# Differential attention on one core: the score pieces of the two maps issued strictly in turn

## The chip, the cores and the metric

The kernel runs on one core of a Trainium2 chip. The metric is the device time of one execution in microseconds (us). The core has a matrix engine (TensorE, in the profile PE for its matmuls and PEld for the loading of its stationary operand), a vector engine (VectorE, DVE), a scalar engine (ScalarE, ACT), GpSimd (POOL), and SyncE (SP), which issues the DMAs. They run side by side and wait for one another by semaphores. SBUF holds operands, PSUM receives what TensorE computes; it has eight banks of 512 float32 values on each of 128 partitions.

## What is computed

One layer of a hybrid network on 128 context tokens and 1024 latent tokens, d_model 1024, all in float32: a SwiGLU feed-forward half step, then differential attention (4 heads, two maps of 64 dimensions each) beside an RG-LRU group, an output projection, and a second feed-forward half step. The attention is this part of the reference:

```python
def block(qi):
    s = jnp.einsum('bqhmd,bkhmd->bhmqk', qi, k, preferred_element_type=jnp.float32) * scale
    p = jax.nn.softmax(s, axis=-1)
    pd = p[:, :, 0] - lam * p[:, :, 1]
    return jnp.einsum('bhqk,bkhv->bqhv', pd.astype(v.dtype), v)
```

A block of 128 queries of one head has two maps of scores, m = 0 and m = 1, each with its own 64 dimensions of the query and the key. Context queries see the 128 context keys; latent queries see 1024 latent keys and 128 keys of a cache.

## The kernel before

All engines run programs written out by hand; the order of the work on each engine is the order of the text, and semaphores tie them together. The feed-forward halves, the projections and the attention follow one another. The attention is the stretch from 1273 to 1508 us of the profile.

It goes over 36 units, u = 0 to 35: for each of four heads one unit of context queries (128 keys) and eight units of latent queries (1152 keys, `UNIT`). For a latent unit `scores(u)` issues six matmuls, which are those of `PIECES`: tuples of map, first key and last key. I call them A1, A2 (map 0, 512 keys each), A3 (map 0, the 128 keys of the cache), and B1, B2, B3 for map 1. In the kernel before their order is A1, A2, B1, A3, B2, B3. In the profile each of these matmuls is two pairs of a weight load and a matmul, so a latent unit has 12 of each; the cache's pieces read `sb_kc`, the others only `sb_x`.

Map 0's operands lie on partitions 0 to 63 and its matmuls are placed at rows 0 to 63 of the array (`tile_position=(m * DH, 0)`), map 1's at rows 64 to 127. Map 0 writes PSUM banks 0 to 2, map 1 banks 3 to 5. There is one set of these banks for all units: ahead of A1 the kernel waits until the exponentials of map 0 of the unit before have been read out of them, ahead of B1 for those of map 1 (`e_done`). After A3 and after B3 `s_ready` is raised.

One pass of the loop on TensorE is: `scores(u)`; then for unit u-2 three transposes of its probabilities, `group(u-2, 0)` (L694); for unit u-3 five blocks of `values` (L708, twice as many records); three more transposes, four more blocks of values, and the last three transposes. The transposes share PSUM bank 6, so each group waits for ScalarE's copy of the one before (`t_done`). ScalarE's pass is: copy of the first transposes of u-2 (L1029), the exponentials of map 0 of unit u (L1036, with the reading of its accumulator as an instruction of its own), second copy, the exponentials of map 1 of unit u, third copy, and the squares of an output (L1044). VectorE's pass is: the maximum over the scores of map 0, that of map 1 (both L1393), the weighted difference of the probabilities of unit u-1 (L1399, L1400, L1402), and the output of u-3 (L1408).

Of the kernel before, what the change touches and what calls it, by code (L numbers as in the profile page):

```python
# [43 lines left out]
GROUP0 = [0] + [1 + 3 * t for t in range(9)]  # L44
GROUPS = GROUP0[9]
UNIT = LAT + 128
PIECES = ((0, 0, 512), (0, 512, 1024), (1, 0, 512), (0, 1024, UNIT), (1, 512, 1024), (1, 1024, UNIT))
MIX_ORDER = (4, 5, 6, 7, 0, 1, 2, 3)
LAM_INIT = 0.8 - 0.6 * math.exp(0.0)
KEYS = T + 128  # L50
# [22 lines left out]
def build(nc, a, out):  # L73
    ctx = ExitStack()
    with ctx:
# [349 lines left out]
        def _(pe):  # L425
# [244 lines left out]
            def scores(u):  # L670

                hd, q = u // QT, u % QT
                for m, b, e in ((0, 0, P), (1, 0, P)) if q == 0 else PIECES:
                    if b == 0 and 2 * u + m > 1:
# [885 lines left out]
```

## Time and profile before

| | |
|---|---|
| runs | 2498.46, 2496.99, 2494.31 us; median 2496.99 |
| the profiled execution | 2498.43 us, of which the span from the first to the last instruction is 2496.6 us |
| attention, 1273 to 1508 us | some 235 us, 36 units |
| PE busy over the span | 2396.6 us (96%) |
| DVE, ACT, POOL busy | 1128.3, 668.6, 29.7 us |
| mean granted TensorE clock | 0.978 |

The profile is one execution. Matmuls are pipelined: a record lasts longer than the distance from one matmul to the next, and a busy PE isn't a PE at its peak. Where the timeline merges records of a kind, "x7" is their number, and the time is that in which at least one of them ran. The bracket at the end of a row tells how long the engine was idle before it, and who released it. The chain of waits follows the end back from what released what.

### The profile page before, as it was taken

Reading aid. Unit: us, or ns where it says so; the run is one execution under the profiler, and the core shown is the slowest. Engines: PE = TensorE matmul, PEld = TensorE weight load, DVE = VectorE, ACT = ScalarE, POOL = GpSimd, SP = SyncE. Lnnn points to the kernel's source line nnn. Section 1 sums busy time; section 2 is a strip of 40 time slices with the busy share of each in tenths; the row PEclk is TensorE's granted clock in tenths of the full one; section 3 lists DMA queues with packets and bytes.
Section 4 is the critical chain, followed back from the end, with each engine's and each line's share of the span. In section 5 each row is a group of like instructions: output and inputs, shape, how many; then the busy total and the mean of one; then the engine's idle time right before and its main releaser. Section 6 shows DMA issues by size and latency. Waiting matters only on the chain.

```text
span 2496.6 us, 35528 instructions
## 1 busy us (share of the span) xinstructions
PE 2396.6 (96%) x14392; PEld 2236.1 (90%) x14392; DVE 1128.3 (45%) x1845; ACT 668.6 (27%) x1174; POOL 29.7 (1%) x36
## 2 busy tenths in 40 slices
PE   5999999999999998999989988999999999999997
PEld 3799999999999987777977768979999999999996
DVE  3544333443334436465557773364443344443335
ACT  3411111111111124465236663251111111111112
POOL 0000000000000000000010030000000000000000
PEclk8999999999999999999989999999999999999998
DMA  9222022210222103111100010111101110101102
GB/s 372 85 75 77 18 83 84 77 74 20 81 84 82 44 1 119 34 34 41 43 21 20 29 46 18 59 52 34 50 22 46 50 50 34 49 22 46 50 9 77
DMA packets 45817, 144.52 MB, mean 58 GB/s; under 512 B 5808, under 2 KB 13360, under 8 KB 45744
## 3 DMA queue, kind: packets, MB, share of 16 engines
q1 hardware_dynamic: 45744, 143.49, 16.7%
q8 instruction: 53, 0.87, 0.1%
q14 instruction: 20, 0.16, 0.0%
HBM read 133.50 MB, written 9.97 MB: 57 GB/s over the span
## 4 chain that ended last, share of the span: by engine, by line
PE 90%; DVE 4%; ACT 3%; DMA 1%; issue 1%; SPq 0%; ACTq 0%; DVEq 0%
PE ps L433 27%; PE ps L435 26%; PE ps L434 26%; PE ps L679 4%; PE ps L708 2%; PE ps L632 2%; DVE sb_tmp L1191 1%; PE ps L694 1%; DVE sb_hL L1183 1%; PE ps L460 1%; DMA sb_stage<-in_w_mod 1%; ACT sb_pr L1036 1%; PE ps L445 1%; PE ps L453 0%; PE ps L470 0%
## 5 line engine op out<-in xcount | busy, mean ns | idle before, releaser
L433 PE MATMUL ps<-sb_hH,sb_guH 128*128 128x384 f32 x2112 | 716.2, 339 | 9.8 <-DVE sb_hL L1183 6.3
L435 PE MATMUL ps<-sb_hH,sb_guL 128*128 128x384 f32 x2112 | 708.0, 335 | 0.0
L434 PE MATMUL ps<-sb_hL,sb_guH 128*128 128x384 f32 x2112 | 708.0, 335 | 0.0
L433 PEld LDWEIGHTS ps<-sb_hH,sb_guH 128*128 128x128 f32 x2112 | 398.0, 188 | 33.7 <-issue 17.4
L1255 DVE SCALAR_TENSOR_TENSOR sb_x<-ps,sb_mod,sb_x 128x128 f32<-128x128 f32 (+1 forms) x704 | 345.9, 515 | 180.9 <-PE ps L435 178.7
L434 PEld LDWEIGHTS ps<-sb_hL,sb_guH 128*128 128x128 f32 x2112 | 398.4, 189 | 0.7 <-issue 0.3
L435 PEld LDWEIGHTS ps<-sb_hH,sb_guL 128*128 128x128 f32 x2112 | 398.3, 189 | 0.0
L1242 DVE TENSOR_TENSOR sb_tmp<-ps,sb_tmp 128x384 f32<-128x384 f32 x132 | 73.5, 557 | 670.6 <-PE ps L435 669.3
L433 PE MATMUL ps<-sb_hidH,sb_dnH 128*128 128x384 f32 x1056 | 356.4, 338 | 0.5 <-DVE sb_x L1255 0.4
L435 PE MATMUL ps<-sb_hidH,sb_dnL 128*128 128x384 f32 x1056 | 353.2, 334 | 0.0
L434 PE MATMUL ps<-sb_hidL,sb_dnH 128*128 128x384 f32 x1056 | 353.1, 334 | 0.0
L895 ACT ACTIVATE sb_hidH<-sb_tmp 128x384 fp32r<-128x384 f32 x132 | 69.3, 525 | 542.4 <-DVE sb_tmp L1242 542.4
L433 PE MATMUL ps<-sb_hH,sb_wiH 128*128 128x384 f32 x576 | 201.6, 350 | 8.3 <-DVE sb_wiL L1104 5.9
L433 PEld LDWEIGHTS ps<-sb_hidH,sb_dnH 128*128 128x128 f32 x1056 | 198.2, 188 | 4.9 <-DVE sb_x L1255 1.0
L892 ACT ACTIVATE sb_tmp<-ps 128x384 f32<-128x384 f32 x132 | 64.4, 488 | 507.0 <-PE ps L435 507.0
L434 PEld LDWEIGHTS ps<-sb_hidL,sb_dnH 128*128 128x128 f32 x1056 | 198.3, 188 | 0.3
L435 PEld LDWEIGHTS ps<-sb_hidH,sb_dnL 128*128 128x128 f32 x1056 | 198.3, 188 | 0.0
L434 PE MATMUL ps<-sb_hL,sb_wiH 128*128 128x384 f32 x576 | 195.9, 340 | 0.0
L435 PE MATMUL ps<-sb_hH,sb_wiL 128*128 128x384 f32 x576 | 195.8, 340 | 0.0
L1104 DVE TENSOR_TENSOR sb_guL<-sb_raw,sb_guH 128x1024 fp32r<-128x1024 f32 x88 | 104.8, 1222 | 66.9 <-ACT sb_guH L795 66.9
L433 PEld LDWEIGHTS ps<-sb_hH,sb_wiH 128*128 128x128 f32 x576 | 110.5, 192 | 16.6 <-issue 5.8
L1393 DVE TENSOR_REDUCE sb_nmx<-ps 128x1 f32<-128x1152 f32 (+1 forms) x72 | 86.3, 1234 | 59.5 <-PE ps L679 58.5
(152 smaller groups left out, 2228.0 us busy)
## 6 DMA issues: line engine op xcount, KB each, us to landing
sb_raw<-in_w_gate SPq DMA_DIRECT2D x44, 512.0 KB, 4.5
sb_raw<-in_w_up SPq DMA_DIRECT2D x44, 512.0 KB, 3.7
sb_raw<-in_w_mod SPq DMA_DIRECT2D x44, 512.0 KB, 4.1
sb_raw<-in_w_down SPq DMA_DIRECT2D x44, 512.0 KB, 4.4
sb_stage<-in_w_mod SPq DMA_DIRECT2D x7, 2048.0 KB, 18.6
sb_raw<-in_w_in SPq DMA_DIRECT2D x16, 512.0 KB, 4.0
sb_x<-in_x SPq DMA_DIRECT2D x3, 1536.0 KB, 10.5
x_spilled<-sb_x SPq DMA_DIRECT2D x8, 576.0 KB, 5.5
```

Of the source, the lines that this page charges most:

```text
L433: pe.matmul(o, wH, xH, start=begin, stop=False)
L434: pe.matmul(o, wH, xL, start=False, stop=False)
L435: return pe.matmul(o, wL, xH, start=False, stop=end)
L632: m = pe.matmul(ps[r, 6 + n % 2, 0:CH], gw[r, w], x[r, XC[j % 2], chunk(c)], start=True, stop=True, tile_position=(r.start, r.start))
L679: mm = pe.matmul(unit(u, m)[:, b:e], x[r, hd, q * P:(q + 1) * P], keys, start=True, stop=True, tile_position=(m * DH, 0))
L708: m = pe.matmul(ps[:, 7, 0:P], pT[:, u % 2, k], vk, start=k == 0, stop=k == nk - 1)
L892: act.activation(tmp[:, b], ps[:, gate_bank(f, c, first)[0], 0:CH], ACT.Silu).then_inc(s["silu"], 1)
L895: act.activation(hidH[:, f, chunk(c)], tmp[:, 2 + b], ACT.Copy).then_inc(s["hidhi"], 1)
L1104: dve.tensor_tensor(dst, raw[:, slot], hi.bitcast(F32), ALU.subtract).then_inc(raw_used[slot], 1)
L1242: dve.tensor_tensor(tmp[:, 2 + b], ps[:, gate_bank(f, c, first)[1], 0:CH], tmp[:, b], ALU.mult).then_inc(s["prod"], 1)
L1255: m = dve.scalar_tensor_tensor(x[:, t, b:e], ps[:, 4 + (c * KT + t) % 3, b - c * CH:e - c * CH], mod[:, gate + t, cond:cond + 1], x[:, t, ...
L1393: dve.tensor_reduce(nmx[:, u % 2, m:m + 1], unit(u, m), AX.X, ALU.max, negate=True).then_inc(mx_ready, 1)
```

## The change

One tuple of constants is reordered. The matmuls, their operands, the PSUM banks and the semaphores are the same; the wait ahead of B1, which stays tied to B1, now stands ahead of A2 as well.

```diff
-PIECES = ((0, 0, 512), (0, 512, 1024), (1, 0, 512), (0, 1024, UNIT), (1, 512, 1024), (1, 1024, UNIT))
+PIECES = ((0, 0, 512), (1, 0, 512), (0, 512, 1024), (1, 512, 1024), (0, 1024, UNIT), (1, 1024, UNIT))
```

In the letters above: A1, A2, B1, A3, B2, B3 becomes A1, B1, A2, B2, A3, B3. The four context units, with one piece for each map, are untouched.

## Rows read from the trace of the kernel before

**Rows 1.** The page: busy time by engine, and the chain's shares by line.
```profile
PE 2396.6 (96%) x14392; PEld 2236.1 (90%) x14392; DVE 1128.3 (45%) x1845; ACT 668.6 (27%) x1174; POOL 29.7 (1%) x36
PE ps L433 27%; PE ps L435 26%; PE ps L434 26%; PE ps L679 4%; PE ps L708 2%; PE ps L632 2%; DVE sb_tmp L1191 1%; PE ps L694 1%; DVE sb_hL L1183 1%; PE ps L460 1%; DMA sb_stage<-in_w_mod 1%; ACT sb_pr L1036 1%; PE ps L445 1%; PE ps L453 0%; PE ps L470 0%
```

**Rows 2.** The chain in the attention, in order of time: start us, us, what.
```profile
1305.95 2.86 PE ps L679 x11
...
1365.63 2.86 PE ps L679 x11
...
1371.68 2.86 PE ps L679 x11
...
1477.01 2.86 PE ps L679 x11
```

**Rows 3.** Timeline of one latent unit: start us, us, engine, line, instruction, count [idle before].
```profile
1366.02 0.22 ACT L1036 ACTIVATION_READ_ACCUMULATOR sb_pr<-ps,sb_nmx 128x1 f32 x1
...
1367.38 0.38 PE L679 MATMUL ps<-sb_kc,sb_x 64*128 64x128 f32 x2
...
1367.80 2.62 DVE L1393 TENSOR_REDUCE sb_nmx<-ps 128x1 f32<-128x1152 f32 x2 [1.38 <-PE ps L679]
1368.11 0.38 PE L679 MATMUL ps<-sb_kc,sb_x 64*128 64x128 f32 x2
...
1368.42 0.31 PEld L694 LDWEIGHTS ps<-sb_ident,sb_pr 128*128 128x128 f32 x3
...
1369.00 0.49 ACT L1029 ACTIVATE sb_pT<-ps 128x384 f32<-128x384 f32 x1 [2.10 <-PE ps L694]
1369.39 1.21 ACT L1036 ACTIVATE sb_pr<-ps,sb_nmx 128x1152 f32<-128x1152 f32 x1
...
1370.95 1.23 ACT L1036 ACTIVATE sb_pr<-ps,sb_nmx 128x1152 f32<-128x1152 f32 x1
```

**Rows 4.** Weight loads of that unit, from short stretches of the timeline.
```profile
1365.56 0.29 PEld L679 LDWEIGHTS ps<-sb_x 64*128 64x128 f32 x2 [0.17 <-issue]
...
1366.29 0.18 PEld L679 LDWEIGHTS ps<-sb_x 64*128 64x128 f32 x1
...
1366.39 0.32 PEld L679 LDWEIGHTS ps<-sb_x 64*128 64x128 f32 x2
...
1366.96 0.19 PEld L679 LDWEIGHTS ps<-sb_kc,sb_x 64*128 64x128 f32 x1
1367.25 0.19 PEld L679 LDWEIGHTS ps<-sb_x 64*128 64x128 f32 x1
...
1368.11 0.19 PEld L679 LDWEIGHTS ps<-sb_kc,sb_x 64*128 64x128 f32 x1 [0.24 <-issue]
```

**Rows 5.** Timeline of the scores of the first latent unit of a head.
```profile
1334.35 2.09 PE L679 MATMUL ps<-sb_x 64*128 64x512 f32 x8
1336.17 0.49 PE L679 MATMUL ps<-sb_kc,sb_x 64*128 64x128 f32 x4
...
1336.59 0.31 PEld L694 LDWEIGHTS ps<-sb_ident,sb_pr 128*128 128x128 f32 x3
```

**Rows 6.** Timeline of the second and third latent units of that head.
```profile
1342.44 2.62 DVE L1393 TENSOR_REDUCE sb_nmx<-ps 128x1 f32<-128x1152 f32 x2 [2.26 <-PE ps L679]
...
1343.84 1.22 ACT L1036 ACTIVATE sb_pr<-ps,sb_nmx 128x1152 f32<-128x1152 f32 x1
...
1345.33 2.26 PE L679 MATMUL ps<-sb_x 64*128 64x512 f32 x6
...
1346.46 0.18 PEld L679 LDWEIGHTS ps<-sb_x 64*128 64x128 f32 x1
```

**Rows 7.** Line 679 from 1358 us on: durations in ns, shortest, median and longest.
```profile
L679 PE MATMUL ps<-sb_x x164: 272/589/693, 1359.5 to 1483.9; 64*128 64x512 f32 x156, 64*128 64x128 f32 x8
```

**Rows 8.** Busy time by stretch: PE, PEld, DVE, ACT, POOL, then granted clock, DMA share, GB/s.
```profile
1277.66:1301.60 23.94, 19.43 (x53) 11.85 (x51) 12.29 (x16) 8.91 (x16) 3.69 (x2) 0.57 0.01 2
1352.80:1356.20 3.40, 3.40 (x11) 2.11 (x8) 1.13 (x1) 0.33 (x3) 0.00 (x0) 0.50 0.00 0
```

## Prediction

> **What bounds the kernel now.** I read the page first. TensorE is busy 96% of the span and carries nearly all of the chain; the scores of the attention (L679) are 4% of it [rows 1]. The change touches these alone, so the question lies in the attention. The chain there shows a pass of 6.05 us for a latent unit (1371.68 less 1365.63; 6.04 by the finer records): 2.86 us of scores and the rest transposes and values, all put down to PE [rows 2]. Read alone, this says that a shorter block of scores shortens the pass one for one. The timeline and the loads say something else, and the prediction rests on the difference.
>
> First, how long do the scores need? The pieces of the two maps sit in different rows of the array. In the first latent unit of a head all eight halves of 512 columns ran within 2.09 us, the four cache halves began 1.82 us after the start, and the next transposes came 2.24 us after it [rows 5]. The halves of one map follow each other by 0.43 us: the second half of A2 is loaded at 1366.53 (1366.39 + 0.32 less a load of 0.18), the first half of A3 at 1366.96 [rows 4]. Eight of them one after another would take 8 x 0.43 = 3.4 us. So in this unit the two maps already run side by side throughout, in the old order, with both 512-column pieces of map 0 ahead of B1 in the text.
>
> Second, why is the usual block 2.86 us and not 2.24? In the unit at 1365.56 the two loads of A1 fall within 0.29 us; a single load starts at 1366.29, 0.73 us after A1, and two more within the 0.32 us from 1366.39 [rows 4]. The load at 1366.29 is that of B1: ScalarE's reading of the accumulator, which ends the exponentials of map 1 of the unit before and frees B1's banks, ended at 1366.02 + 0.22 = 1366.24 [rows 3], 0.05 us ahead. It isn't held by A2, whose second half is loaded later. The kinds of the loads confirm that one map passes the other: a cache load (A3) at 1366.96, then one of 512 columns (of map 1) at 1367.25, and the last cache load (B3) at 1368.11 [rows 4]. B1 is late by a wait on ScalarE, and the profile shows no idle time for it because A1 keeps PE busy.
>
> Third, what closes the pass. From B1 at 1366.29 the stream of map 1 runs to the transposes at 1368.42; then come the first copy on ScalarE at 1369.00, the exponentials of map 0 at 1369.39, a second copy, and the exponentials of map 1 from 1370.95 [rows 3]. Their accumulator read ends one pass after the last one, 1366.24 + 6.04 = 1372.28, and 0.05 us later the next B1 can start: 1372.33, just 6.04 us after 1366.29. ScalarE closes the loop, and B1's start is its other end.
>
> **The change part by part.** It removes and adds no instruction, no transfer and no wait, and no queue but TensorE's has anything moved. Three things move.
>
> B1 is issued ahead of A2. It can't start earlier: in the usual unit it starts 0.05 us after the event it waits for, and that event hangs on ScalarE's chain, which the change doesn't shorten. In the unit at 1334.35, where nothing holds it, both maps end together already. Gain 0.
>
> B2 is issued ahead of A3; B3 stays last. In the free unit the four cache halves take 0.49 us [rows 5] where the two of one map take 0.38 [rows 3], so map 1 ends 0.11 us behind map 0. If that is B2 standing too far back, 0.11 us of TensorE goes away; but what ends late in this unit is ScalarE's work on map 0. Gain 0 to 0.11 us in each of three such units, 0.3 in all; I take 0.
>
> A2 now stands behind B1's wait. Queued with it are B2, A3, B3 and the transposes; who waits for A2 and A3 is VectorE's maximum of map 0, and then the exponentials of map 0. Today A2's second half is loaded at 1366.53, one step of 0.43 after its first half, which is thus loaded at 1366.10 and runs from 1366.53. After the change its load comes behind the two of B1, which are 0.10 apart (1366.29, 1366.39): at 1366.50 at the best. It is in time but not hidden: a first matmul, whose load is uncovered, lasts 693 ns and the others 589 [rows 7], 0.10 us for the load. So A2 is late by 1366.50 + 0.10 - 1366.53, some 0.1 us. Lower bound 0 (it starts when it did); upper bound 0.3 us, if A2 gets in only with B1's second half, 0.43 + 0.10 us after B1, at 1366.82. What covers it: the two maxima run from 1367.80 for 2.62 us, the first to some 1369.15, and the exponentials that need it start at 1369.39, held by the first copy [rows 3]. Less a hand-over of 0.04 the cover is 0.20 us. A delay of 0.1 costs nothing here. At 0.3 it costs 0.10 us in each unit of this pattern, which is the chain's block of 2.86 us, seen from 1305.95 to 1477.01 [rows 2], in about 20 of the 32 latent units: 2.0 us.
>
> The cover is missing in one kind of unit, the second latent one of a head. There the first maximum ends at 1342.44 + 1.35 = 1343.79 and the exponentials of map 0 start at 1343.84; the next unit starts at 1345.33, and its B1 is loaded only at 1346.46, 1.13 us later [rows 6], behind the exponentials of map 1, which hang on the second maximum. Here the 0.1 us goes straight into the loop: 3 x 0.1 = 0.3 us. In the third unit itself A2 would start behind B1, at 1.13 + 0.2 and an uncovered load instead of at 0.96, some 0.5 us late; its exponentials are held by the first copy, which comes as much later as B1 does (0.4 us), so with the cover of 0.2 nothing is left to pay.
>
> Sum: 0 + 0 + 0 + 0.3 = 0.3 us, on the profiled execution 2498.43 + 0.3 = 2498.7. That execution lies 1.44 us above the median of the runs, so the median after is 2496.99 + 0.3 = 2497.3 us.
>
> **A rule against the trace.** B1's first half is loaded at 1366.29 and A2's second half only at 1366.53 [rows 4]: one map overtakes the other. The Trainium skill (TensorE: Matmul & The Clock Gate, "Part 3: Packing small matmuls — row/col tiling") holds that between row groups only weight loads are pulled ahead and that matmuls keep their order in start and end. What it would make of the change is rival 1; the trace does not agree with it.
>
> **The rivals.** 1. Faster: matmuls keep the order of the text, so A2 holds B1 today. Then B1 begins no earlier than A2's second half, whose load at 1366.53 puts its matmul at 1366.53 + 0.43 = 1366.96, and the change moves B1 to 1366.29. It would give back 0.67 us in each of 20 usual units, 13.4 us, and 1.39 (A2's second half from the start of a block) in each of three free ones, 4.2: 17.6 us, 2479 us. For it: only the text's order. Against it: the free block of 2.24 us [rows 5] has no room for a late B1, and in the usual unit the loads of map 1 fall between those of map 0. 3 in 100.
>
> 2. Slower: the array takes alternating pieces in lockstep, so that with B1 held for 0.73 us the rest of map 0 is held with it. A3 then ends 0.11 us ahead of B3; today A3 is at 1367.38 and B3 at 1368.11 [rows 3], so A3 is late by 0.73 - 0.11 = 0.62. Above the cover of 0.20 this costs 0.42 us in each of 20 units, 8.4 us, and 0.62 in each of three, 1.9: 2507 us. It decides from a delay of 0.20 us, and passes 5 us from some 0.40. For it: A2 is now behind the wait, and nothing in the trace shows a piece of map 0 that is needed at once behind a wait of map 1. Against it: right behind B1's wait the loads go out 0.10 apart. 5 in 100.
>
> 3. The clock. From 1277.7 to 1301.6 us the mean granted clock is 0.57, mostly at 1.2 instead of 2.4 GHz, while TensorE waits again and again as the attention begins; from 1352.8 to 1356.2 it is at the lower level once more, after the start of a new head [rows 8]. One such spell of 3.4 us costs 1.7 us. The change leaves TensorE's work and gaps nearly as they are. One spell more or less is 1.7 us either way and belongs to the scatter. 2 in 100 that it makes 5 us or more, shared between the signs.
>
> **How the numbers follow.** A measurement of this kernel can tell about 0.2%, 5.0 us, from no change; its runs lie within 4.2 us. The forecast, no change that can be told, has 90 in 100; faster 3 + 1 = 4; slower 5 + 1 = 6. The range goes from 2497.3 upward by 2.0 for the upper bound of A2's delay, 1.7 for a spell of the clock and 0.5 for scatter of the median, to 2501.5; downward by 0.3 + 0.3 for the second and first latent units, 1.7 for a spell and 1.7 for scatter, to 2493.3. The rivals beyond it hold less than 2 in 10.
>
> **What would show it.** In the profile after: usual passes still 6.04 us; B1's load still 0.73 us after A1 and 0.05 after the accumulator read; the maximum of map 0 at 2.24 to 2.35 us after A1 (today 1367.80 less 1365.56); the exponentials of map 0 still behind the first copy; the free unit's block 2.1 to 2.3 us. It is wrong if that maximum starts later than 2.45 us after A1 and the pass grows by the excess, or if the pass falls below 6.0 us, which would mean that B1 was held by something other than ScalarE.

## The result, and the profile after

The changed kernel takes 2510.68 us (median of 5 runs, 2504.68 to 2511.3), the one before 2496.99 us (2492.86 to 2498.46). The ratio is 1.0048 with a 95% interval of 1.0035 to 1.0061: slower by 9 to 15 us. The forecast was 2497.3 us and no change that can be told. Two later executions, one of each kernel, took 3138 and 11762 us at a mean granted clock of 0.71 and 0.18 and enter no figure here.

The profiled execution took 2511.08 us with a span of 2509.3 us, 12.7 us more than before. From the first scores to those of the last unit, 35 passes on, it goes from 209.9 us (1273.12 to 1482.98) to 223.8 us (1270.36 to 1494.13), 13.9 us more. The attention begins 2.8 us earlier, though nothing ahead of it was changed (3.4 us less at the lower clock there account for some 1.7 of it, by an estimate), and what follows is 1.6 us longer.

The timeline of one usual latent unit, starting at 1317.59 us, in the changed kernel:

```profile
1317.59 0.29 PEld L679 LDWEIGHTS ps<-sb_x 64*128 64x128 f32 x2 [0.17 <-issue]
1317.59 2.28 PE L679 MATMUL ps<-sb_x 64*128 64x512 f32 x7
1318.05 0.21 ACT L1036 ACTIVATION_READ_ACCUMULATOR sb_pr<-ps,sb_nmx 128x1 f32 x1
...
1318.32 0.72 PEld L679 LDWEIGHTS ps<-sb_x 64*128 64x128 f32 x5 [0.43 <-ACT sb_pr L1036]
...
1319.41 0.38 PE L679 MATMUL ps<-sb_kc,sb_x 64*128 64x128 f32 x2
...
1319.71 0.59 PE L679 MATMUL ps<-sb_x 64*128 64x512 f32 x1
1320.14 0.38 PE L679 MATMUL ps<-sb_kc,sb_x 64*128 64x128 f32 x2
...
1320.35 2.62 DVE L1393 TENSOR_REDUCE sb_nmx<-ps 128x1 f32<-128x1152 f32 x2 [1.71 <-PE ps L679]
...
1321.03 0.49 ACT L1029 ACTIVATE sb_pT<-ps 128x384 f32<-128x384 f32 x1 [2.10 <-PE ps L694]
1321.74 1.22 ACT L1036 ACTIVATE sb_pr<-ps,sb_nmx 128x1152 f32<-128x1152 f32 x1 [0.22 <-DVE sb_nmx L1393]
...
1323.97 0.69 PE L679 MATMUL ps<-sb_x 64*128 64x512 f32 x1
```

Against [rows 3]: the matmuls run as they did. A3 begins 1.82 us after A1 (1319.41 less 1317.59; before 1367.38 less 1365.56), B3 2.55 us after it, the same as before; A2 isn't late at all. But the maximum of map 0, which waits for A3 alone, starts 2.76 us after A1 instead of 2.24. The exponentials of map 0 no longer follow the first copy, which ends at 1321.52; ScalarE idles 0.22 us until the maximum is there. The pass is 6.38 us (1323.97 less 1317.59) instead of 6.04.

The chain of that unit names the new link, VectorE's maximum, where before it held PE alone [rows 2]:

```profile
1317.66 2.67 PE ps L679 x8
...
1320.35 1.37 DVE sb_nmx L1393
...
1321.74 1.31 ACT sb_pr L1036 x2
1323.06 0.39 ACT sb_pT L1029
...
1323.49 0.55 PE ps L694 x3
```

So: scores, maximum, exponentials of map 0, second copy, last transposes. The question is why a matmul that ran when it always did is reported half a microsecond later.

### The profile page after: what moved, and what is told of

Its sections match the earlier page's. It is cut to its first block, busy times and chain, and to the rows that moved or that the text cites. A ratio compares the mean times of both kernels' runs of the same rounds, so it can differ in the third digit from the quotient of the medians.

```text
span 2509.3 us, 35528 instructions
## 1 busy us (share of the span) xinstructions
PE 2404.8 (96%) x14392; PEld 2237.8 (89%) x14392; DVE 1127.4 (45%) x1845; ACT 671.3 (27%) x1174; POOL 29.6 (1%) x36
## 4 chain that ended last, share of the span: by engine, by line
PE 89%; DVE 5%; ACT 3%; DMA 1%; issue 1%; SPq 0%; ACTq 0%; DVEq 0%
PE ps L433 27%; PE ps L435 26%; PE ps L434 26%; PE ps L679 4%; ACT sb_pr L1036 2%; DVE sb_nmx L1393 2%; PE ps L632 1%; DVE sb_tmp L1191 1%; DVE sb_hL L1183 1%; PE ps L460 1%; DMA sb_stage<-in_w_mod 1%; PE ps L694 1%; PE ps L708 1%; PE ps L445 1%; PE ps L470 1%
## 5 line engine op out<-in xcount | busy, mean ns | idle before, releaser
L433 PE MATMUL ps<-sb_hH,sb_wiH 128*128 128x384 f32 x576 | 201.5, 350 | 9.2 <-DVE sb_wiL L1104 5.7
```

The lines of the kernel that those rows point to most:

```text
L433: pe.matmul(o, wH, xH, start=begin, stop=False)
```

## The experiments

Two theories stood after the traces had been compared. S: the end of a matmul, and with it the semaphore that it raises, is told in the order of the text even where a later one ran first, so that A3's signal waits for B2, now issued ahead of it. In the rows above the last 512-column half, B2's, begins at 1319.71 and lasts 0.59: 1320.30, and VectorE starts at 1320.35. W: the cost comes from A2 and all behind it standing behind B1's wait.

**Each half of the change alone.** The differences below are written with the letters of the pieces in place of their tuples. Only A3 and B2 back in their old order, with A2 still behind the wait:

```diff
-PIECES = (A1, B1, A2, B2, A3, B3)
+PIECES = (A1, B1, A2, A3, B2, B3)
```

> Order A1, B1, A2, A3, B2, B3: against the changed kernel only A3 and B2 are swapped, and A2 still stands behind B1's wait. Theory S (a matmul's end is told in program order, so that the signal behind A3 waits until B2, issued ahead of it, is through): nothing that ends late stands ahead of A3, so the maximum of map 0 starts 2.24 us after A1 as in the kernel before, the usual pass is 6.04 us, and the time about 2497 us (2493 to 2501). Rival W (what costs is that A2 and all behind it stand behind B1's wait): maximum at 2.76, pass 6.38, time 2508 to 2511 as in the changed kernel.

Only A3 and B2 swapped against the kernel before, with A2 ahead of the wait:

```diff
-PIECES = (A1, A2, B1, A3, B2, B3)
+PIECES = (A1, A2, B1, B2, A3, B3)
```

> Order A1, A2, B1, B2, A3, B3: against the kernel before only A3 and B2 are swapped, and A2 stands ahead of B1's wait. Theory S: the signal of map 0 comes with the end of B2, 2.12 + 0.59 + 0.05 = 2.76 us after A1, the usual pass is 6.38 us, the time 2507 to 2511. Rival W: as before, 2.24 us, 6.04 us and about 2497 us. A third view, that the array itself runs A3 later when it is issued later, would show A3's records later than 1.82 us after A1.

The first: 2496.51 us, ratio to the kernel before 0.9996 (0.9987 to 1.0006). The second: 2505.84 us, 1.0037 (1.0023 to 1.0051). The same rows of a usual unit, first of A1, B1, A2, A3, B2, B3:

```profile
1363.03 2.28 PE L679 MATMUL ps<-sb_x 64*128 64x512 f32 x7
...
1364.85 0.38 PE L679 MATMUL ps<-sb_kc,sb_x 64*128 64x128 f32 x2
...
1365.14 0.59 PE L679 MATMUL ps<-sb_x 64*128 64x512 f32 x1
1365.27 2.62 DVE L1393 TENSOR_REDUCE sb_nmx<-ps 128x1 f32<-128x1152 f32 x2 [1.38 <-PE ps L679]
...
1369.07 0.69 PE L679 MATMUL ps<-sb_x 64*128 64x512 f32 x1
```

and of A1, A2, B1, B2, A3, B3:

```profile
1369.24 2.28 PE L679 MATMUL ps<-sb_x 64*128 64x512 f32 x7
...
1371.06 0.38 PE L679 MATMUL ps<-sb_kc,sb_x 64*128 64x128 f32 x2
...
1371.35 0.59 PE L679 MATMUL ps<-sb_x 64*128 64x512 f32 x1
...
1372.00 2.62 DVE L1393 TENSOR_REDUCE sb_nmx<-ps 128x1 f32<-128x1152 f32 x2 [1.71 <-PE ps L679]
...
1375.61 0.69 PE L679 MATMUL ps<-sb_x 64*128 64x512 f32 x1
```

In both A3 begins 1.82 us after A1 and B2's last half 2.11. Where A3 is issued ahead of B2 the maximum starts 2.24 us after A1, 0.04 behind A3's end and in the middle of B2; where it is issued behind, 2.76 us, 0.06 behind B2's end. Passes: 6.04 and 6.37. W falls: the wait ahead of A2 costs nothing that a measurement tells. S's starts and passes came in both; its time came for the first, and for the second 2505.84 us lies 1.2 us below the 2507 to 2511 expected. The third view, that the array begins A3 later, falls with the unchanged 1.82.

It isn't VectorE that is late either. The traces hold the moment at which a semaphore changes: `s_ready` is raised for map 0 2.22 us after A1 in the kernel before and in A1, B1, A2, A3, B2, B3, and 2.74 us after it in the changed kernel and in A1, A2, B1, B2, A3, B3; the maximum follows 0.02 us later in all four.

**The dose.** B2 in two pieces of 256 columns, the second behind A3:

```diff
-PIECES = (A1, B1, A2, B2, A3, B3)
+PIECES = (A1, B1, A2, (1, 512, 768), A3, (1, 768, 1024), B3)
```

> The changed order with B2 cut into two pieces of 256 columns, the second one moved behind A3: A1, B1, A2, B2 first half, A3, B2 second half, B3; one more matmul (two more pairs). Theory S: the signal of map 0 waits only for the 256-column piece, which begins 1.69 us after A1 and ends about 2.28, so the maximum starts at 2.28 to 2.35 us, within the cover of 0.20 us: pass 6.04 to 6.10, time 2496 to 2501. Rival W: maximum at 2.76, pass 6.38, 2508 to 2511.

2497.23 us, 1.0004 (0.9993 to 1.0015). The unit:

```profile
1358.46 2.06 PE L679 MATMUL ps<-sb_x 64*128 64x512 f32 x7
...
1360.36 0.38 PE L679 MATMUL ps<-sb_x 64*128 64x256 f32 x1
...
1360.79 2.62 DVE L1393 TENSOR_REDUCE sb_nmx<-ps 128x1 f32<-128x1152 f32 x2 [1.38 <-PE ps L679]
...
1364.51 0.69 PE L679 MATMUL ps<-sb_x 64*128 64x512 f32 x1
```

The shorter piece ahead of A3 ends at 1360.36 + 0.38 = 1360.74, and the maximum starts 0.05 us later, 2.33 us after A1. That is 0.09 us later than in the kernel before and inside the cover of 0.20; the pass is 6.05 us. So the delay follows the piece that is issued ahead, and it is covered as the prediction said.

**All of map 0 first.**

```diff
-PIECES = (A1, A2, B1, A3, B2, B3)
+PIECES = (A1, A2, A3, B1, B2, B3)
```

> Order A1, A2, A3, B1, B2, B3: nothing of map 1 stands ahead of any piece of map 0. Theory S: the maximum of map 0 at 2.24 us after A1, pass 6.04 us, about 2497 us, and a little less (by up to 1 us) where map 1 is held longest. Rival W: the same, 2497 us. What it tells apart is how far map 1 may overtake: B1 now has five halves of map 0 between itself and the first instead of three. If it can't reach past them, the block of the first latent unit of a head grows from 2.24 us towards 2.6 or more and the usual pass grows too.

2512.61 us, 1.0058 (1.0042 to 1.0075), the slowest of all. S and W had both said 2497; the test of the reach decided it. The maximum of map 0 is at 2.24 us after A1 as S wants. But B1 begins late, in the free first latent unit of a head too. Its loads, and behind them those of the free unit at 1334.35 in the kernel before:

```profile
1339.28 0.29 PEld L679 LDWEIGHTS ps<-sb_x 64*128 64x128 f32 x2 [0.17 <-issue]
1339.82 0.19 PEld L679 LDWEIGHTS ps<-sb_x 64*128 64x128 f32 x1 [0.24 <-issue]
1340.24 0.30 PEld L679 LDWEIGHTS ps<-sb_x 64*128 64x128 f32 x3 [0.24 <-issue]
```

```profile
1334.35 0.31 PEld L679 LDWEIGHTS ps<-sb_x 64*128 64x128 f32 x4 [0.17 <-issue]
1334.89 0.19 PEld L679 LDWEIGHTS ps<-sb_x 64*128 64x128 f32 x1 [0.23 <-issue]
1335.32 0.30 PEld L679 LDWEIGHTS ps<-sb_x 64*128 64x128 f32 x3 [0.24 <-issue]
```

Before 1340.24 there are two loads of A1 and one of A2; B1's comes right behind the next, 0.97 us after A1 by the finer records, when A2 has just begun. In the kernel before four loads, two of them B1's, lie in the first 0.3 us of such a unit. This pass is 6.29 us (1345.57 less 1339.28; 5.85 in the kernel before), and so is the usual one (6.04). In the profiled execution two spells of 10.2 us at the lower clock stand behind the third latent units of two heads. The passes at full clock are worth some 6 us by the records; what else the 15 us hold wasn't taken apart.

**What limits the reach.** In the kernel before B1 overtakes three halves that haven't begun; with map 0 whole ahead of it, it waits until three are left. A1 cut in two puts six halves of map 0 ahead of B1, the first four of them of 256 columns:

```diff
-PIECES = (A1, A2, B1, A3, B2, B3)
+PIECES = ((0, 0, 256), (0, 256, 512), A2, B1, A3, B2, B3)
```

> The order of the kernel before with A1 cut into two pieces of 256 columns, so that six halves of map 0 stand ahead of B1 instead of four. With map 0 issued whole (also six ahead) B1 began in a free unit only when the third half had begun, 0.97 us after A1. If what limits the overtaking is a number of waiting matmuls (at most three may stand unbegun ahead), B1 begins with the third of the shorter halves, about 0.53 us after A1. If it is a time or a number of columns, it begins at 0.97 as there.

One execution of each took 2497.73 us and, for the kernel before, 2496.09 us. In the free unit at 1332.30 us the loads within some 0.3 us are two, and the next three lie within 0.40 us of 1332.62:

```profile
1332.30 0.29 PEld L679 LDWEIGHTS ps<-sb_x 64*128 64x128 f32 x2 [0.17 <-issue]
...
1332.62 0.40 PEld L679 LDWEIGHTS ps<-sb_x 64*128 64x128 f32 x3
```

By the records B1 begins 0.54 us after A1, together with the third half, as a count of three unbegun matmuls ahead says; a time would have given 0.97. Nor is it a number of columns: at 0.54 us 1280 of them stood unbegun ahead of B1 here, and with as many it was still held there. The loads of the kernel before fit too: in the free unit B2's first load comes 0.97 us after A1 (among the three from 1335.32), when A2's first half has begun and its second and the two of A3 are left. That load is uncovered (B2's first half lasts 0.69 us), and this is the 0.11 us by which map 1 ended behind map 0 there; in the changed kernel, with B2 ahead of A3, it is 0.01.

**The link that closes the loop.** The second copy (L1029) sits between the two exponentials on ScalarE. It goes to VectorE, behind its maxima, with both orders of the scores (the definition of `second_copy` is left out):

```diff
                 exps(u, 0)
-                p_copy(u - 2, 1)
                 exps(u, 1)
...
                     for m in range(2):
                         maxima(u, m)
+                second_copy(u - 2)
```

> The order of the kernel before; the copy of the second group of transposes (1, between the exponentials of map 0 and of map 1) goes from ScalarE to VectorE, behind its two maxima. If ScalarE's chain closes the pass (first copy, exponentials of map 0, second copy, exponentials of map 1, B1 of the next unit), the exponentials of map 1 start right behind those of map 0, some 5.1 instead of 5.39 us after A1, B1 comes 0.3 us earlier, and the usual pass falls from 6.04 to 5.75 us: 2490 to 2494 us. If TensorE alone sets the pass, it stays at 6.04 and the time at 2497. It gets slower if VectorE's copy (0.5 to 0.6 us) comes too late for the third group of transposes.

> The same move of the second copy, in the changed order A1, B1, A2, B2, A3, B3. Theory S: the maximum of map 0 still waits for B2 (2.04 us after B1's load), the pass is 0.3 us longer than in the same kernel with the old order: about 6.1 us, 2498 to 2504 us. If the 0.33 us of the change came from the second copy being late, and not from the first maximum, the two orders would now be equal.

With the old order: 2485.41 us, 0.9954 (0.9937 to 0.9971), faster than both kernels. With the changed order: 2496.79 us, 1.0006 (0.9994 to 1.0018). A usual unit with the old order, then one with the changed order:

```profile
1359.48 2.38 PE L679 MATMUL ps<-sb_x 64*128 64x512 f32 x8
...
1361.72 2.62 DVE L1392 TENSOR_REDUCE sb_nmx<-ps 128x1 f32<-128x1152 f32 x2 [0.73 <-PE ps L679]
...
1364.26 0.55 DVE L1415 COPY sb_pT<-ps 128x384 f32<-128x384 f32 x1
1364.38 1.22 ACT L1036 ACTIVATE sb_pr<-ps,sb_nmx 128x1152 f32<-128x1152 f32 x1
...
1364.86 0.31 PEld L694 LDWEIGHTS ps<-sb_ident,sb_pr 128*128 128x128 f32 x3 [0.16 <-DVE sb_pT L1415]
```

```profile
1362.99 2.38 PE L679 MATMUL ps<-sb_x 64*128 64x512 f32 x8
...
1365.43 2.62 DVE L1392 TENSOR_REDUCE sb_nmx<-ps 128x1 f32<-128x1152 f32 x2 [0.93 <-PE ps L679]
...
1366.82 1.22 ACT L1036 ACTIVATE sb_pr<-ps,sb_nmx 128x1152 f32<-128x1152 f32 x1 [0.22 <-DVE sb_nmx L1392]
```

The exponentials of map 1 start 4.90 us after A1 instead of 5.39, so ScalarE's chain did close the pass. The pass falls to 5.86 us and not to the 5.75 expected: VectorE's copy at 1364.26 now holds the third transposes for 0.16 us, a new link. The time fell by 12 us where 3 to 7 were expected. In the attention (first scores to the last unit's) the profile shows 201.5 us instead of 209.9; about half of these 8.4 us are shorter passes and the rest is less time at the lower clock at its start and behind the transition of 1352 us. In the changed order the maximum starts 2.44 us after A1, 0.05 behind B2's end (1362.99 + 2.38 = 1365.37), and the pass is 6.06. The cover is gone, so the 0.20 us of delay cost 0.20 us of pass (0.3 were expected; B1, and B2 with it, come earlier here). The delay itself doesn't come from the copy, and the difference between the orders stays: 11.4 us between the medians. Of these, 0.20 in some 17 usual passes and 0.19 and 0.71 in the second and the third latent unit of three heads make 6.1 us; the rest stands beside more time at the lower clock in the attention, 27.3 us against 10.2 in the profiled executions, and wasn't separated. The time of the changed order, 2496.79 us, lies 1.2 us below the 2498 to 2504 expected.

**The changed kernel once more**, on the same chip as these two:

> The changed kernel once more, beside the others on one chip. Theory S: maximum of map 0 at 2.76 us, pass 6.38 us; 20 usual passes at 0.33 us and about 0.85 us for the second and third latent units of three heads give 9 us, and the rest of its 12 us is time at the lower clock behind the third latent unit, which may or may not be there in a given execution: ratio 1.003 to 1.006.

2506.18 us, 1.0036 (1.002 to 1.0053). Usual passes of 6.38 us again, and the profiled execution (2511.52 us) has its spells at the lower clock where that of the first measurement has them: 1351.99, 1410.02 and 1464.63 us, against 1351.98, 1410.01 and 1464.62.

## Why the prediction was wrong

*What bounds the kernel.* Right. Both maps run side by side in the old order, ScalarE closes the loop, B1 starts 0.05 us behind the accumulator read before and after the change (1318.05 + 0.21, load at 1318.32), and moving the second copy shortened the pass.

*B1 ahead of A2: gain 0.* Right. B1's start in the usual unit is at 0.73 us with it ahead of A2 and behind it.

*A2 behind the wait: 0.1 us late, covered.* Harmless as said: A2's records begin 0.96 us after A1 in the usual unit, so it was late by 0, the lower bound. Its load went out beside B1's first, at 1318.32, and was hidden behind A1's second half, so the 0.10 us for an uncovered load wasn't due, and neither were the 3 x 0.1 us in the second latent units that made up the whole sum: this pass is 5.12 us in A1, B1, A2, A3, B2, B3 as in the kernel before. In the third latent unit of the changed kernel A2 was late, its first half by 0.3 us (it begins with B1, 1.27 us after A1), its second half and A3 by 0.4. This cost nothing by itself: with A3 back ahead of B2 that pass is 6.46 us, as before.

*B2 ahead of A3: gain 0 to 0.11.* This is the step that failed. Its gain was read rightly (in the free unit the transposes start 2.14 us after A1 instead of 2.24, and the pass stays 5.86), but its cost was put at nothing without a reason: it looked at what B2 gains and not at who now stands behind B2. A3 carries the signal of map 0, and its end is reported no earlier than B2's: 0.52 us late (2.76 less 2.24), 0.20 covered, some 0.33 us left in each of about 17 usual passes, 5.6 us. The second and the third latent unit, without cover, cost 0.40 and 0.46 us in each of three heads, 2.6 us. Together 8.2 us. The first head's slow start took 1.7 us more, which makes 9.9, but that part isn't shown to come from this step: with A1 cut in two, where A3 stands ahead of B2, the stretch from the first scores to the first usual pass took 34.1 us, against 32.8 in the kernel before and 34.5 in the changed one. The order A1, A2, B1, B2, A3, B3, which differs from the kernel before by this step alone, measured 9 us (6 to 13). The sign of being wrong that the prediction named came as written: the maximum at 2.76 us, later than 2.45, and the pass grown by the excess, 0.33.

*The cover of 0.20 us.* Right. 0.09 of delay cost 0.01 us of pass, 0.52 cost 0.33, and without the cover 0.20 cost 0.20.

*The rival for slower.* It had the place (the maximum of map 0 exceeds the cover), a delay of 0.62 against 0.52 measured, and a price of 10 us against 9 to 15. That it came so near is luck: its mechanism was wrong, since the array isn't in lockstep and A3 wasn't late at all. It was weighed on when loads go out and matmuls begin, and I never asked in what order they are reported.

*The rule against the trace.* The Trainium skill (TensorE: Matmul & The Clock Gate, "Part 3: Packing small matmuls — row/col tiling") says that matmuls keep their order in start and end. The starts in this case don't: B1 begins 0.73 us after A1, A2 0.96 us. The ends are reported in order, as the five starts of the maximum above show. The recorded ends aren't in order (A3's at 2.20, B2's at 2.71 in the changed kernel), but the profiler models these. I threw the rule out whole on the evidence of its first half. Its second half, with the starts left as the trace had them, gives the 0.52 us of delay.

The trace of the kernel before held the answer in one place. In the third latent unit B1 is held to 1.13 us and stands ahead of A3:

```profile
1347.00 0.19 PEld L679 LDWEIGHTS ps<-sb_x 64*128 64x128 f32 x1
1347.15 0.38 PE L679 MATMUL ps<-sb_kc,sb_x 64*128 64x128 f32 x2
...
1347.64 2.62 DVE L1393 TENSOR_REDUCE sb_nmx<-ps 128x1 f32<-128x1152 f32 x2 [0.53 <-PE ps L679]
```

The load at 1347.00 marks the beginning of B1's second half, which lasts 0.59: 1347.59. The maximum of map 0 starts at 1347.64, 2.31 us after A1 (1345.33 [rows 6]) and 0.11 behind A3's end at 1347.53, where in all other units it is 0.04 behind. Seven hundredths of a microsecond, in a unit in which nothing waited for them.

*What stays open.* Whether A3 itself finishes late or only its report is held back, no run tells; what waits for it starts at the same time either way.

The profiled execution lost 13.9 us in the attention, of which 9.9 are named above. The rest, 4 us, lies in the passes with spells at the lower clock, more than the one spell of 1.7 us that the prediction allowed. The changed kernel shows them behind the third latent unit of each of three heads, the kernel before of one. Granted clock (third figure from the end) in the second and the third head, first of the changed kernel, then of the kernel before:

```profile
1346.03:1367.70 21.67, 19.64 (x101) 14.61 (x101) 14.58 (x20) 12.20 (x27) 0.00 (x0) 0.84 0.00 1
1402.50:1423.80 21.30, 19.09 (x102) 13.28 (x102) 14.64 (x20) 12.36 (x27) 0.00 (x0) 0.92 0.00 1
```

```profile
1345.33:1365.56 20.23, 18.84 (x102) 14.01 (x101) 14.75 (x20) 11.86 (x27) 0.00 (x0) 0.92 0.00 1
1398.98:1417.50 18.52, 17.12 (x102) 13.06 (x101) 14.64 (x20) 11.84 (x27) 0.00 (x0) 1.00 0.00 1
```

TensorE idled 1.87 us in the third latent unit's pass, which leads up to such a spell, against 1.40 before; but with 1.73 us of idling the order A1, A2, B1, B2, A3, B3 had none of these spells in its profiled execution, and with 1.41 us the order A1, B1, A2, A3, B2, B3 had two. These are single executions. Of the changed kernel there are two, with the same three spells, and both are among its longer ones: its 13 times lie in two clusters, seven from 2503.0 to 2508.3 us at a mean granted clock of 0.977 to 0.980 and six from 2510.7 to 2512.0 at 0.975 or 0.976, as if the spells came in some and not in others. The lower cluster, by its middle time of 2504.7, is 7 to 8 us above the kernel before, near the 8.2 worked out above. Only 4 of 43 times of the kernel before lie above 2501 us, none above 2503. So the changed kernel seems to fall into these spells more often; what brings them wasn't settled.

## What to carry to other kernels

Where matmuls in different rows of the array overtake each other, read two orders: in this kernel they began when their operands and rows were free, within a short reach, and were reported in the order of the text. Put the matmul whose semaphore someone waits for ahead of everything that needn't be done first, and cost a reordering by who stands behind each piece, not only by what the moved piece gains. A matmul's record doesn't show when its end was reported; the semaphore, and the start of the instruction that waits for it, do.

## What the runs showed of the hardware

The instruction that waits for a matmul started 0.04 to 0.06 us after the latest recorded end among it and the matmuls issued ahead of it, and the semaphore itself was raised 0.02 us before that start: starts at 2.24, 2.33, 2.44 and 2.76 us after A1 as the piece ahead of A3 ended at 1.85, 2.28, 2.38 and 2.71, while A3 itself began at 1.82 us each time. (In the first case A3's own end, 2.20, was the latest.)

A matmul of the free rows began while at most three issued ahead of it hadn't begun. With four halves of the other map ahead, B1 began 0.01 us after the first; with six, it waited for the third, 0.97 us where they had 512 columns and 0.54 where the first four had 256. The second figure is from one profiled execution. That reach is why the order of the kernel before works, and why passes grew where one map was issued whole, a kernel slower by 0.6% in all.
